# Output projection of a hybrid attention step: seven half-size products per unit in place of eight, with their weight and operand sums on DVE and POOL

## The reference

```
xn = rms_norm(x, norm_g)
h  = xn @ w_in                       # all branches: q, k, v, u, gates ga and gb
oa = sparse top-k attention          # 8 heads of 64
ob = stick-breaking attention        # 8 heads of 64
ya = (oa * silu(ua)) @ w_a_out       # 512 -> 1024
yb = (ob * silu(ub)) @ w_b_out       # 512 -> 1024
mixed = sigmoid(ga) * ya + sigmoid(gb) * yb
y  = x + mixed @ w_o                 # 1024 x 1024: the output projection
```

## Time and profile before

| what | us |
|---|---|
| median of 3 runs (lowest, highest) | 525.01 (524.34, 526.58) |
| profiled execution: its own time | 523.65 |
| its span, first to last instruction | 521.9 |
| PE busy in the span | 515.1 |
| mix stage | 421.28 to 469.44 |
| output stage, mix's end to last matmul | 469.44 to 519.11 |

### The profile page before, as it was taken

The page is one execution under the profiler, slowest core; times in us unless marked ns, Lnnn a source line. Parts: engine busy times, 40 slices in busy tenths (PEclk is TensorE's granted clock), DMA queues, the critical chain, the costliest instruction groups (busy, mean ns, idle before and its releaser), DMA issues.

```text
span 521.9 us, 10124 instructions
## 1 busy us (share of the span) xinstructions
PE 515.1 (99%) x4188; PEld 485.5 (93%) x4188; DVE 370.7 (71%) x718; ACT 258.2 (49%) x434; POOL 76.7 (15%) x73
## 2 busy tenths in 40 slices
PE   8999999999999999999999999999999999999997
PEld 6889999999998988989998888999999999999997
DVE  5878758899979989478857668563987556665331
ACT  7655764344366566864244665653566532231100
POOL 3506000014034314284000000000000000000000
PEclk9999999999999999999999999999999999999999
DMA  7623305142331322023230016020232172245111
GB/s 274 266 80 123 92 1 167 35 168 82 117 133 28 140 82 82 1 82 122 87 113 4 1 47 212 2 82 1 82 105 98 42 252 80 82 162 189 50 52 46
DMA packets 15359, 50.45 MB, mean 97 GB/s; under 512 B 2288, under 2 KB 6000, under 8 KB 11728
## 3 DMA queue, kind: packets, MB, share of 16 engines
q1 hardware_dynamic: 15168, 49.49, 27.6%
q10 hardware_dynamic: 144, 0.30, 0.2%
HBM read 42.82 MB, written 6.82 MB: 95 GB/s over the span
## 4 chain that ended last, share of the span: by engine, by line
PE 91%; DVE 4%; issue 2%; ACT 2%; DMA 1%; ACTq 0%
PE PS L665 40%; PE PS L1004 9%; PE PS L958 8%; PE PS L989 8%; PE PS L619 4%; PE PS L784 3%; PE PS L765 3%; PE PS L649 3%; PE PS L869 2%; PE PS L741 2%; PE PS L710 2%; PE PS L849 1%; PE PS L690 1%; PE PS L598 1%; PE PS L793 1%
## 5 line engine op out<-in xcount | busy, mean ns | idle before, releaser
L665 PE MATMUL PS<-xhi,whi 128*128 128x272 f32 x320 | 94.6, 296 | 0.0
L665 PE MATMUL PS<-xlo,whi 128*128 128x272 f32 x320 | 92.4, 289 | 0.0
L665 PE MATMUL PS<-xhi,wlo 128*128 128x272 f32 x320 | 92.1, 288 | 0.0
L1452 DVE TENSOR_TENSOR wlo<-raw,whi 128x2048 fp32r<-128x2048 f32 (+1 forms) x31 | 64.5, 2080 | 17.3 <-ACT whi L1051 15.9
L665 PE MATMUL PS<-whi,xhi 128*128 128x256 f32 x256 | 73.4, 287 | 0.8 <-DVE nmx L1844 0.8
L665 PE MATMUL PS<-wlo,xhi 128*128 128x256 f32 x256 | 72.4, 283 | 0.0
L665 PE MATMUL PS<-whi,xlo 128*128 128x256 f32 x256 | 71.9, 281 | 0.0
L665 PEld LDWEIGHTS PS<-xhi,whi 128*128 128x128 f32 x320 | 60.3, 189 | 2.9 <-issue 2.3
L1051 ACT ACTIVATE whi<-raw 128x2048 fp32r<-128x2048 f32 (+1 forms) x31 | 52.1, 1682 | 18.2 <-PE PS L1004 18.2
L665 PEld LDWEIGHTS PS<-xhi,wlo 128*128 128x128 f32 x320 | 60.4, 189 | 0.0
L665 PEld LDWEIGHTS PS<-xlo,whi 128*128 128x128 f32 x320 | 60.2, 188 | 0.0
(11 more groups left out here) (283 smaller groups left out, 1318.2 us busy)
## 6 DMA issues: line engine op xcount, KB each, us to landing
raw<-in_w_units SPq DMA_DIRECT2D x28, 1024.0 KB, 4.9
raw<-in_w_mixes SPq DMA_DIRECT2D x8, 512.0 KB, 3.4
stage<-in_x_kw_qi SPq DMA_DIRECT2D x7, 564.5 KB, 5.1
res<-in_x_kw_qi SPq DMA_DIRECT2D x1, 2176.0 KB, 8.1
out<-res SPq DMA_DIRECT2D x16, 136.0 KB, 1.7
out<-vals SPq DMA_DIRECT2D x2, 1024.0 KB, 6.2
out<-kT SPq DMA_DIRECT2D x1, 1088.0 KB, 8.7
out<-tm SPq DMA_DIRECT2D x1, 1024.0 KB, 8.0
```

What stands on the lines that cost most here:

```text
L665: mm = pe.matmul(out, lhsT, rhs, start=(k == 0), stop=(k == 23))
L1452: dve.tensor_tensor(wlo[:, uu % 2, 0:n], raw[:, uu % 2, 0:n], whi[:, uu % 2, 0:n].bitcast(F32), ALU.subtract).then_inc(w_lo, 1)
```

## The change

The output projection is done like the fast gates: per unit seven products of 12 matmuls. With it:

- `FIRST_OUT` gives unit 0 another order of products (p1, p2, p4, p5, p6, p3, p7) and a fourth bank; units 1 to 3 keep `PRODUCTS`.
- Weight sums t1, t3, t2, t4: POOL for unit 0 (`out_sums`), which also makes unit 0's low parts (`first_low`); DVE for units 1 to 3 (`later_sums`), placed in its queue between the adds of the unit before. Slot 0 serves units 0 and 2, slot 1 units 1 and 3.
- Operand sums s1 to s4 of the mixed activations, per pair of chunks: POOL for pairs 0 to 2 (`pair_sums`), DVE for the last (`sum_m`); their high parts on ACT, their low parts on DVE.
- The adds into `res` are eight for unit 0 and seven for each later unit; p6, p3, p7 (and p4 of units 1 to 3) wait for an add.
- Mix counts three events per d, so that DVE multiplies branch b while PE does branch a; d = 7 is finished half by half.
- `res` is four tensors in the place of gates 0, 1, 4 and 5 with a DMA each; the loads of out0 to out3 have other places and other waits in SP's queue.

The diff, cut to its core (`-` before, `+` after):

```diff
+M_FORMS = ("s1", "s2", "s4", "s3")
+LAST_SUMS = {"s3": 1, "s1": 2, "s2": 3, "s4": 4}
+
+
+
+FIRST_OUT = [("p1", "b11", "x11", "a"), ("p2", "b21", "x12", "c"), ("p4", "t4", "x22", "d"), ("p5", "t1", "s1", "b"),
+             ("p6", "t2", "s2", "a"), ("p3", "b22", "s4", "b"), ("p7", "t3", "s3", "a")]
+OUT_BANKS = [{"a": 4, "b": 5, "c": 6, "d": 7}, {"a": 0, "b": 1, "c": 2}]
+FIRST_TAKEN = [("p1", 0, 0), ("p2", 0, 0), ("p4", 0, 1), ("p5", 1, 1), ("p6", 1, 0), ("p3", 1, 0), ("p7", 0, 1), ("p7", 1, 1)]
+LATER_TAKEN = [("p1", 0, 0), ("p5", 1, 1), ("p6", 1, 0), ("p3", 1, 0), ("p7", 1, 1), ("p2", 0, 0), ("p4", 0, 1)]
+
+
...
+            def load_out(o):
+                uu = U[f"out{o}"]
+                if o == 0:
+                    sp.wait_ge(f_lo_done, len(PARTS) * len(FAST))
+                elif o == 1:
+                    sp.wait_ge(w_lo, direct_index(U["mix7"]) + 1)
+                elif o == 2:
+                    sp.wait_ge(y_lo_first, len(PARTS))
+                else:
+                    sp.wait_ge(y_lo_done, len(PARTS) * (o - 2))
+                sp.dma_start(raw_of(uu), w_units[big_index(uu)]).then_inc(out_raw[o % 2], 16)
+
...
+            def load_res(o):
+
+                if o < 3:
+                    sp.wait_ge(ms_summed, o + 1)
+                else:
+                    sp.wait_ge(ms_last, len(M_FORMS))
+                sp.wait_ge(m_lo, (1, 2, 5, 6)[o])
+                e = UC // P * o
+                sp.dma_start(res[o], x_kw_qi.rearrange("c p n -> p c n")[:, e:e + UC // P, 1:FIRST_AT]).then_inc(out_res[o], 16)
...
-            for name, _ in UNITS[U["gate2"]:]:
+            for name, _ in UNITS[U["gate2"]:U["mix2"]]:
                 load_unit(name)
-                if name == "mix2":
-                    sp.wait_ge(f_done, len(PRODUCTS) * len(FAST))
...
+            load_out(0)
+            for name, _ in UNITS[U["mix2"]:U["out0"]]:
+                load_unit(name)
+            load_res(0)
+            load_res(1)
+            load_out(2)
+            load_out(1)
+            load_res(2)
+            load_res(3)
+            load_out(3)
+            for o in range(OUTS):
+                seen = {(f, h): k for k, (_, f, h) in enumerate(out_taken(o))}
+                for (f, h), k in sorted(seen.items(), key=lambda v: v[1]):
+                    sp.wait_ge(y_added, taken_by(o, k))
+                    sp.dma_start(y_fm[:, UC // P * o + f, halved(h)], res[o][:, f, halved(h)]).then_inc(st_y, 16)
...
-                mm.then_inc(mix_done, 1)
+                        if br == 0 or h == 1:
+                            mm.then_inc(mix_done, 1)
...
-            for g in range(3, 2 * KC):
-                if g % 4 == 0:
-                    pe.wait_ge(w_lo, direct_index(U[f"out{g // 4}"]) + 1)
-                if g >= 8:
-                    pe.wait_ge(y_out, g - 7)
-                out_group(g, range(KC)).then_inc(y_done, 1)
+            def out(o):
+
+                banks = OUT_BANKS[o % 2]
+                for n, form, block_, b in out_products(o):
+                    part = [form in p for p in PARTS].index(True)
+                    if o == 0:
+                        pe.wait_ge(y_lo_first, (0, 2, 3, 1)[part] + 1)
+                    else:
+                        pe.wait_ge(y_lo_done, len(PARTS) * (o - 1) + (0, 2, 3, 1)[part] + 1)
+                    if n == "p1":
+                        if o >= 2:
+                            pe.wait_ge(y_added, taken_by(o - 1, -1))
+                        else:
+                            pe.wait_ge(mix_used, D // P - 1 + o)
+                    elif n in ("p5", "p2") and o >= 2:
+                        pe.wait_ge(y_added, taken_last(o - 2, "p3" if n == "p5" else "p2"))
+                    elif n == "p6":
+                        pe.wait_ge(y_added, taken_last(o, "p1"))
+                    elif n == "p3":
+                        pe.wait_ge(y_added, taken_last(o, "p5"))
+                    elif n == "p7":
+                        pe.wait_ge(y_added, taken_last(o, "p6"))
+                    elif n == "p4" and o >= 1:
+                        pe.wait_ge(y_added, taken_last(o, "p7"))
+                    opens = n in ("p1", "p5", "p2") or b == "d"
+                    for c in range(KC // 2):
...
+                        for k, (a, w) in enumerate(PASSES):
+                            q = QUARTER * FORMS[form]
+                            wt = by(KC // 2, (slots_hi, slots_lo)[w][o % 2][:, q:q + QUARTER])
+                            mm = pe.matmul(ps[:, banks[b], 0:HALF_NT], wt[:, c, :], m_block(a, block_, c),
+                                           start=(opens and c + k == 0), stop=(c == KC // 2 - 1 and k == 2),
+                                           skip_group_check=True)
+                    mm.then_inc(y_done, 1)
+
+            for o in range(OUTS):
+                out(o)
 
...
+            def out_high(o, part):
...
+                if part == 0:
+                    act.wait_ge(out_raw[o % 2], 16 * (o // 2 + 1))
+                    if o == 0:
+                        act.wait_ge(f_done, len(PRODUCTS) * len(FAST))
+                    elif o == 1:
+                        act.wait_ge(mix_done, 3 * D // P)
+                    else:
+                        act.wait_ge(y_done, len(PRODUCTS) * (o - 1))
...
             for d in range(D // P):
+                if d == D // P - 1:
+                    for h in range(2):
+                        act.wait_ge(mixed, d + 1 + h)
+                        act.activation(mhi[:, d, halved(h)], gates[d][:, 0, halved(h)], ACT.Copy).then_inc(m_hi, 1)
+                        if h == 0:
+                            sum_high_m(2)
+                    sum_high_m(3)
+                    break
                 act.wait_ge(mixed, d + 1)
-                act.activation(mhi[:, d, :], gates[d][:, 0, :], ACT.Copy).then_inc(m_hi, 1)
-                w_high(f"mix{d + 2}" if d + 2 < D // P else f"out{d + 2 - D // P}")
-            for o in range(2, D // UC):
-                w_high(f"out{o}")
+                n = HALF_NT if d in K_HALVES[0] else NT
+                act.activation(mhi[:, d, 0:n], gates[d][:, 0, 0:n], ACT.Copy).then_inc(m_hi, 1)
+                if d + 2 < D // P:
+                    w_high(f"mix{d + 2}")
+                if d in (1, 2):
+                    for part in ((0, 3), (1, 2))[d - 1]:
+                        out_high(0, part)
+                elif d in (4, 5):
+                    sum_high_m(d - 4)
+            for o in range(1, OUTS):
+                for part in (0, 3, 1, 2):
+                    out_high(o, part)
...
-            for d in range(D // P):
...
+            def sum_low_m(pair, form):
+
+                dve.wait_ge(ms_high, m_form(pair, form))
+                dve.tensor_tensor(m_block(1, form, pair), m_sum(form, pair), m_block(0, form, pair).bitcast(F32),
+                                  ALU.subtract).then_inc(ms_low, 1)
...
+            def m_low(d, lo, hi, count):
+
+                dve.wait_ge(m_hi, count)
+                dve.tensor_tensor(mlo[:, d, lo:hi], gates[d][:, 0, lo:hi], mhi[:, d, lo:hi].bitcast(F32),
+                                  ALU.subtract).then_inc(m_lo, 1)
...
+            for d in range(D // P - 1):
+                dve.wait_ge(mix_done, 3 * d + 1)
                 if d <= EARLY_GATES:
                     dve.wait_ge(gates_sig, 2 * (EARLY_GATES + 1))
                 else:
                     dve.wait_ge(f_sig, d - EARLY_GATES)
...
+                gated(d, 1, None)
+                dve.wait_ge(mix_done, 3 * d + 3)
+                gated(d, 0, None).then_inc(mix_used, 1)
                 dve.wait_ge(mix_used, d + 1)
                 dve.tensor_tensor(gates[d][:, 0, :], gates[d][:, 0, :], gates[d][:, 1, :], ALU.add).then_inc(mixed, 1)
-                dve.wait_ge(m_hi, d + 1)
-                dve.tensor_tensor(mlo[:, d, :], gates[d][:, 0, :], mhi[:, d, :].bitcast(F32), ALU.subtract).then_inc(m_lo, 1)
-                w_low(f"mix{d + 2}" if d + 2 < D // P else f"out{d + 2 - D // P}")
-
-            dve.wait_ge(res_in, 16)
-            for g in range(2 * KC):
-                e, h = divmod(g, 2)
-                dve.wait_ge(y_done, g + 1)
-                v = res[:, e, halved(h)]
-                dve.tensor_tensor(v, v, ps[:, OUT_BANK[g % 8], 0:HALF_NT], ALU.add).then_inc(y_out, 1)
-                if g % 4 == 3 and g // 4 + 2 < D // UC:
-                    w_low(f"out{g // 4 + 2}")
+                m_low(d, 0, HALF_NT if d in K_HALVES[0] else NT, d + 1)
+                if d + 2 < D // P:
+                    w_low(f"mix{d + 2}")
+                if d in (4, 5):
+                    for form in M_FORMS:
+                        sum_low_m(d - 4, form)
+            d = D // P - 1
+            dve.wait_ge(mix_done, 3 * d + 1)
+            dve.wait_ge(f_sig, d - EARLY_GATES)
+            link(gated(d, 1, None))
+            dve.wait_ge(mixed, d)
+            sum_m("s3")
...
+            for h in range(2):
+                dve.wait_ge(mix_done, 3 * d + 2 + h)
```

(116 more changed lines are left out.)

159 lines of the change are left out of this document (118 added, 41 removed).

## The result

Four runs of each kernel, in turn on one chip: before 524.67 us (524.03 to 526.58), changed 530.47 us (530.18 to 531.45). The ratio is 1.0111, 95% interval 1.0084 to 1.0137: slower by 1.1%, outside the predicted range. The profiled execution of the changed kernel took 531.45, span 529.6, mean granted clock 0.990; the other three had spans of 528.4 to 528.7 and 0.994. So the two profiled executions lie further apart (7.7 us of span) than the medians (5.8).

What follows compares the result with a forecast made beforehand. PE was taken as the bound, busy 515.1 of 521.9 us. An output stage 1.5 us shorter after p3's waits, against 1.5 us of POOL meetings, summed to 0.0: 525.0 us, range 523.0 to 528.0.

Steps and rivals of the forecast that it cites:

- the saving of 7.1: Output stage: 28 products take 42.56 us in place of 49.67, if PE never waited.
- p3's waits: Output stage: PE waits before p3 for p5's add in DVE's queue, 2.9 in unit 0 and 2.7 for units 1 and 2.
- mild meetings: POOL and DVE holding each other off at the shared SBUF port, together 1.5 us, bounds 0 to 4.4.
- A product is 1.52 us: Output stage: each product costs PE 1.52 us, taken from two fast gates of seven products each.
- p3's waits of units 1 and 2, 1.35 each: Output units 1 and 2: p3 starts 1.35 us late per unit, behind p5's add on DVE.
- p3's wait of unit 0, 2.9: Output unit 0: PE wants p3 7.60 us after mix's end and gets it at 10.5, a 2.9 us wait.
- I took 0.2, of 0 to 0.6: Output unit 0: `pair_sums(2)` meets the last chunk's DVE work and delays the queue by 0.2 us.
- One boundary later the delay is 1.1 ... I take 0.9: Mix 0: POOL's sums hold up DVE's last four low parts; PE delayed 0.9 us, cases 0, 1.1, 2.1.
- The second meeting: Mix 3: POOL's `first_low` and `pair_sums` hold up DVE, delaying mix 5 by 0.4 us, bounds 0 and 1.7.
- The clock as a rival at 0.16: Unit 0's p3 wait lowers PE's clock, adding 1.5 to 2.5 us: 526.5 to 527.5, chance 0.16.
- 3 to 5 us: After a clock fall in unit 0's p3 wait, PE would run some 3 to 5 us at half speed.
- the rival on POOL: POOL holds DVE off in mix, meetings cost over 4.1 us: 527.7 to 528.5, chance 0.13.

Runs made afterwards that it cites:

- e8: Changed kernel with DVE's weight sums for output units 1 to 3 cut to 8 columns, parts made from raw weights; 524.00 us.
- e3: Changed kernel with every POOL tensor_tensor pass of the stage replaced by a write of zeros; 524.16 us.
- e4: Changed kernel with 24 unread matmuls on PE ahead of the wait before p3 of unit 0; 528.53 us.
- e1: Changed kernel with POOL's weight sums of unit 0 held until DVE has made the gated h's low parts; 526.36 us.
- e2: Changed kernel with DVE's later sums split and placed around the adds, parts of units 1 to 3 reordered; 525.39 us.
- e10: e6 with the next mix weights' parts made ahead of the mixed rows' parts on ACT and DVE; 519.38 us.
- e7: Changed kernel with the weight sums of all four output units on POOL, DVE keeping adds and low parts; 527.49 us.
- e9: e4 plus nine unread matmuls ahead of each of the two waits in the first mix product; 527.87 us.
- e5: Changed kernel with the edits of e1 and e2 together; 521.74 us.
- e6: e5 with ACT making unit 0's high parts one mix product earlier; 521.10 us.

## Why the prediction was wrong

Forecast: the saving of 7.1 eaten by p3's waits (5.6) and by mild meetings (1.5), sum 0.0. Measured between the profiles: +7.7. The difference by steps:

- **A product is 1.52 us: right** (1.506).
- **p3's waits of units 1 and 2, 1.35 each: right** (1.29 and 1.30), placed and released as said; e8 shows that the sums on DVE cause them.
- **p3's wait of unit 0, 2.9: mis-sized**, 3.69, and 0.8 of short waits beside it. The step behind it is POOL's share in that queue: I took 0.2, of 0 to 0.6, for `pair_sums(2)` alone. In e3, where POOL reads nothing, p3 starts 10.67 after mix's end, as my count on DVE said (10.5); in the changed kernel 11.78. So POOL's share was 1.1. From mix's end `later_sums(1)` started at 8.05 and not at 6.7. The output stage without the fall of the clock is 49.29 (e4), where I had 48.2 and 0.2: +0.9.
- **"One boundary later the delay is 1.1 ... I take 0.9": failed.** All three POOL passes got in, with 2.48 of waits, above even the bound of 2.1 that I gave. DVE worked without a pause there and POOL took each boundary, which is what the earlier trace rows had shown; I chose the middle where the row pointed at the end. e1 shows the cause by removing it. The passes were also longer than their prices, 2.40, 1.29 and 1.30 (e1) where I took 2.00 and 1.1 from an operation of another kind.
- **The second meeting, 0.4 of 0 to 1.7: mis-sized**: 0.8 at mix 5 and 0.5 at mix 7, which I had only in the rival. Mix without the fall of the clock (e2, which has the same waits: its mix is 52.34, 1.3 shorter) is 4.2 longer than before; I took 0.9 + 0.4: +2.9.
- **The clock as a rival at 0.16, at nothing in the sum: failed.** My own row had the clock fall 2.4 us after PE's last matmul, and my own sum had PE stand still for 2.9. The fall was therefore part of the likeliest case, or near it: by the clocks it came in all four executions of the changed kernel and in three of six of e1. In the profile it fell about 2.6 us into the wait (3.81 us at a mean of 0.86, the end of them at 0.50) and cost 2.56 by e4. The "3 to 5 us" at half speed that I gave it are not in the rows named with them; it was 5.8 behind the wait, from 486.72 to 492.50. The second fall, in mix, I had not thought of: 1.3. Together +3.9.

0.9 + 2.9 + 3.9 = 7.7, as measured. So neither rival alone decided. The meetings in mix cost 4.2, at the edge of the "over 4.1" that the rival on POOL wanted, and the clock fell as well: both came true together, which I had given no chance of their own. e3 gives what POOL's reading costs in all, 5.46 in mix and 2.22 in output, the whole of the difference: with a POOL that only writes, the two stages are as long as before, though p3 of unit 0 still waits and 13 matmuls behind it are slow (24 in the changed kernel). Open: what sets whether the clock falls in mix, and why three of e1's six executions show no fall at all.

## What to carry to other kernels

Work given to an idle POOL isn't free where both engines read two SBUF operands and DVE has no pause: charge every POOL pass nearly in full to DVE's queue (here 4.4 of 5.0 us), then ask what in that queue PE waits for, and put that first (e10 hides 26 us of POOL in mix in this way). Where a step of your sum gives PE a wait about as long as one behind which a row shows the clock lower, the fall belongs in the sum, with its chance. An in-order queue ahead of a bank handover wants the add first and the long passes behind it; moved once, the passes stood ahead of another add, that of p1 in the next unit (e2).

## What was not expected of the hardware

The clock's fall is not tied to one long wait. In the changed kernel PE stopped for 1.24 us twice, with three matmuls between, and 11 matmuls behind were spaced 0.226. The same two waits stand in five profiles: the changed kernel, e4 and e8 show the fall (mix 53.6 to 53.8), e2 and e7 don't (52.3), and e9, with the waits filled, is at 52.37. A wait of 1.76 alone before p6 of unit 1 (e2, e5, e6, e10) left the clock at 1.00 each time; those of 3.1 to 3.8 before p3 or p4 of unit 0 didn't in any profile (changed, e1, e3, e7). Filler matmuls kept it up in both places (e4, e9) and gained what the slow matmuls had cost, by the ratios 0.3% and 0.4% of this kernel.

The same kernel can have a fall in one execution and not in the next. Of the executions without a trace only the mean clock and the span are on record. A clock of 0.997 goes with a fall in mix (profiles of e4, e8), 0.994 with one before p3 (e1), 0.990 with both. By that the changed kernel had the fall in mix once in four, e2 five times in ten, e4 twice in four, e8 six times in ten, e9 never in five. This isn't certain, as a fall elsewhere looks the same: e3's profile has one far from the change (a mean of 0.61 between 26 and 30 us), and the kernel before had 0.996 and 0.997 in two of 21 executions. An execution at 1.000 had none at all: e1, whose wait before p3 is 3.69 in the profile as in the changed kernel, had three such, 2.7 to 3.0 us shorter than its others. One fall more or less moves an execution by 1.3 to 3 us, which is as much as most of the experiments move the kernel.
